# Two layers of a hybrid decoder on one core: the first stage of each layer with its ring of logits held in the banks

## The reference

```
h_n    = x * rsqrt(mean(x*x) + eps) * gain          # normalised rows
logits = einsum(q_idx, k_idx / 8)                   # 8 heads of 64, both rotated
score  = einsum(w * 8**-0.5, relu(logits))          # weighted sum over the 8 heads
idx    = top_k(where(causal, score, -inf), 128)
g      = -exp(a_log) * softplus(a + dt_bias);  gam = cumsum(g);  beta = sigmoid(b)
q,k,v  = silu(causal_conv(proj))                    # 4 taps
```

## Time and profile before

| | us |
|---|---|
| median of 3 runs (2298.42 to 2299.43) | 2298.96 |
| the profiled execution | 2299.94 |
| its span | 2298.2 |
| TensorE matmul busy | 2239.7 (97%) |
| VectorE busy | 1174.5 (51%) |
| ScalarE busy | 1000.6 (44%) |
| GpSimd busy | 1126.9 (49%) |

### The profile page before, as it was taken

One profiled execution on the slowest core, in us unless ns is written; L12 is line 12 of the kernel. 1 busy time (PEld: TensorE's weight loads), 2 busy tenths in 40 slices (PEclk: granted clock), 3 DMA queues, 4 the chain that ended last, 5 costly groups with the idle time before them and its releaser, 6 DMA issues.

```text
span 2298.2 us, 32941 instructions
## 1 busy us (share of the span) xinstructions
PE 2239.7 (97%) x12820; PEld 1834.3 (80%) x12820; DVE 1174.5 (51%) x2175; ACT 1000.6 (44%) x2237; POOL 1126.9 (49%) x824
## 2 busy tenths in 40 slices
PE   8999998999999999999999999999999999999998
PEld 6788887888788888888867888878887888888886
DVE  7778776544522344440186788754445324444302
ACT  5555655455522433332355455545544324333322
POOL 4366445333345555554445566443443555555542
PEclk9999999999999999999999999999999999999999
DMA  4211211222233333333322221112222333333332
GB/s 152 65 53 55 61 56 38 69 74 75 68 96 97 94 99 97 97 96 96 90 71 69 56 56 56 51 43 74 75 77 73 97 97 92 96 97 97 98 98 88
DMA packets 98939, 183.36 MB, mean 80 GB/s; under 512 B 11104, under 2 KB 11360, under 8 KB 98784
## 3 DMA queue, kind: packets, MB, share of 16 engines
q1 hardware_dynamic: 98784, 181.26, 27.3%
HBM read 179.12 MB, written 2.10 MB: 79 GB/s over the span
## 4 chain that ended last, share of the span: by engine, by line
PE 85%; DVE 10%; ACT 3%; issue 1%; POOL 1%; DMA 0%; DVEq 0%; SPq 0%; ACTq 0%; POOLq 0%
PE bank L1530 82%; PE bank L1597 2%; DVE conv_acc L1005 1%; DVE left L1005 1%; DVE normalised L1005 1%; PE bank L1875 1%; DVE bank L1002 1%; DVE ob_lo L1002 1%; ACT w_hi L596 1%; DVE left L1205 1%; POOL mt_even L535 0%; DVE iq L1002 0%; DVE inv L1002 0%; PE bank L1591 0%; ACT oa_hi L607 0%
## 5 line engine op out<-in xcount | busy, mean ns | idle before, releaser
L495 POOL TENSOR_TENSOR w_lo<-w_raw,w_hi 128x512 fp32r<-128x512 f32 x668 | 931.9, 1417 | 1071.9 <-ACT w_hi L596 1071.9
L1530 PE MATMUL bank<-xn_hi,w_lo 128*128 128x512 f32 x1840 | 747.5, 406 | 0.0
L1530 PE MATMUL bank<-xn_hi,w_hi 128*128 128x512 f32 x1840 | 739.1, 402 | 6.6 <-DVE conv_acc L1005 6.6
L1530 PE MATMUL bank<-xn_lo,w_hi 128*128 128x512 f32 x1840 | 731.0, 397 | 0.0
L596 ACT ACTIVATE w_hi<-w_raw 128x512 fp32r<-128x512 f32 x668 | 385.0, 624 | 653.6 <-PE bank L1530 648.9
L1530 PEld LDWEIGHTS bank<-xn_hi,w_hi 128*128 128x128 f32 x1840 | 348.0, 189 | 84.3 <-DVE conv_acc L1005 9.1
L1530 PEld LDWEIGHTS bank<-xn_hi,w_lo 128*128 128x128 f32 x1840 | 348.2, 189 | 72.5 <-issue 5.8
L1530 PEld LDWEIGHTS bank<-xn_lo,w_hi 128*128 128x128 f32 x1840 | 348.0, 189 | 68.5 <-issue 1.9
L1002 DVE TENSOR_TENSOR residual<-residual,bank 128x512 f32<-128x512 f32 x32 | 22.0, 686 | 252.8 <-PE bank L1530 252.4
L1530 PE MATMUL bank<-mid_hi,w_hi 128*128 128x512 f32 x352 | 136.9, 389 | 0.0
L1530 PE MATMUL bank<-mid_lo,w_hi 128*128 128x512 f32 x352 | 136.9, 389 | 0.0
(11 more groups left out here) (262 smaller groups left out, 3460.5 us busy)
## 6 DMA issues: line engine op xcount, KB each, us to landing
w_raw<-w_tiles SPq DMA_DIRECT2D x668, 256.0 KB, 2.6
residual<-x_t SPq DMA_DIRECT2D x4, 512.0 KB, 5.7
out_t<-normalised SPq DMA_DIRECT2D x8, 256.0 KB, 2.1
rope<-rope SPq DMA_DIRECT2D x2, 512.0 KB, 5.8
mats<-mats SPq DMA_DIRECT2D x1, 576.0 KB, 3.9
vecs_all<-vecs SPq DMA_DIRECT2D x1, 129.0 KB, 7.7
mats<-mats SPq DMA_DIRECT2D x1, 128.0 KB, 6.8
vecs_all<-vecs SPq DMA_DIRECT2D x1, 4.0 KB, 1.8
```

Source lines behind the costliest of these rows:

```text
L495: nc.gpsimd.tensor_tensor(w_lo[j][:], w_raw[j][:], w_hi[j][:].bitcast(F32), ALU.subtract).then_inc(s_lo, 1)
L1530: return nc.tensor.matmul(out, lhsT, rhs, start=start, stop=stop)
```

## The change

The buffers `irl` go. Relu now works in place in the bank, the adds read the bank, and TensorE waits for the add of the group before instead of its Relu. The keys of tile 0 go to bank 3 and the spread root to bank 0 (they change places). The normalised rows read the root from the bank instead of `row_r`; rows 0 and 2 are written to banks 4 and 5, and so the first logits wait for `lo2`. Front tile 0 (bank 0) waits for `y7`. Rows 6 and 7 and the adds of 512 columns in group 0 change places with other steps. The decays stand behind the adds of group 1 and convolution 1, Ln behind the tanh of convolution 1 and the tap of convolution 2, and TensorE issues 36 products instead of 6 before `cum`. Columns of the head and the masks follow convolution 3, the gate's row product follows convolution 5. Tile 0's products are issued half by half with all products of the high weight first (`low_last`), and at the start ScalarE makes the high copies 2 to 5 between the squares instead of ahead of them. Left out below are the lists of step names, which follow the new order, and lines in which only the bank's number changes.

```diff
 ab_col = sb("ab_col", [NC, 16], at=slot(42) + 512)
-irl = [sb(f"irl_{j}", [SEQ], at=slot(44 + j)) for j in range(HGROUP)]
...
+SPREAD, KEYS = 0, 3
...
+def scaled_in(k):
...
+    return bank[{0: 4, 2: 5}[k]][:] if k in (0, 2) else sq[:, k, :]
...
+def square_in(k):
...
+    return bank[SPREAD if k == KEYS else k][:]
...
     def square(k):
-        dst = squares[:, k, :] if k in (0, KD - 2) else bank[k][:]
+        dst = squares[:, k, :] if k in (0, KD - 2) else square_in(k)
...
             act.wait_ge(rms_v.sem, rms_v.after(turn, f"y{k}"))
-            copy(xn_hi[:, k, :], sq[:, k, :]).then_inc(rms_a.step(f"hi{k}"), 1)
+            copy(xn_hi[:, k, :], scaled_in(k)).then_inc(rms_a.step(f"hi{k}"), 1)
...
         def relus(g, t):
-            before = GROUPS.index((g, t)) - 1
             for i in heads_of(g):
-                j, n = i % HGROUP, (t + 1) * P
+                logit = bank[2 + i % HGROUP][:, :(t + 1) * P]
                 act.wait_ge(idx_p.sem, idx_p.after(l, f"lg{t}_{i}"))
-                if before >= 0:
-                    bg, bt = GROUPS[before]
-                    act.wait_ge(idx_v.sem, idx_v.after(l, f"acc{bt}_{bg * HGROUP + j}"))
-                nc.scalar.activation(irl[j][:, :n], bank[2 + j][:, :n], ACT.Relu).then_inc(idx_a.step(f"relu{t}_{i}"), 1)
+                nc.scalar.activation(logit, logit, ACT.Relu).then_inc(idx_a.step(f"relu{t}_{i}"), 1)
...
         w_hi_after(l, 4)
+        relus(0, 3)
         rms_hi(l, 6, 7)
-        relus(0, 3)
...
         relus(1, 1)
-        act.wait_ge(idx_v.sem, idx_v.after(l, "u"))
-        nc.scalar.activation(small[:, 7, :], small[:, 4, :], ACT.Ln).then_inc(idx_a.step("ln"), 1)
...
         relus(1, 3)
+        tile_done(l, T0_GDN + 2)
+        w_hi_after(l, T0_GDN + 2)
+        front_tanh(l, 0, 1)
+        front(l, 0, 2, False, split_next=False)
+        act.wait_ge(idx_v.sem, idx_v.after(l, "u"))
+        nc.scalar.activation(small[:, 7, :], small[:, 4, :], ACT.Ln).then_inc(idx_a.step("ln"), 1)
+        tile_done(l, T0_GDN + 3)
+        w_hi_after(l, T0_GDN + 3)
...
         nc.scalar.activation(col_total[:], small[:, 10, :].rearrange(by_head, c=NC), ACT.Exp).then_inc(idx_a.step("etot"), 1)
-        tile_done(l, T0_GDN + 2)
-        w_hi_after(l, T0_GDN + 2)
-        front_tanh(l, 0, 1)
-        front(l, 0, 2, False, split_next=False)
...
             w_hi_through(k // 3)
-    w_hi_through(3)
...
         square(k)
-        if k == 3:
-            w_hi_through(4)
+        if k % 2:
+            w_hi_through(2 + k // 2)
...
                 head_rest(l, 0)
-            tile_done(l, T0_GDN + m + 1)
-            w_hi_after(l, T0_GDN + m + 1)
+            if m > 2:
+                tile_done(l, T0_GDN + m + 1)
+                w_hi_after(l, T0_GDN + m + 1)
...
         into = KD - 2 if k == KD - 1 else 0
-        tt_(squares[:, into, :], squares[:, into, :], bank[k][:], ALU.add).then_inc(rms_v.step(f"sum{k}"), 1)
+        tt_(squares[:, into, :], squares[:, into, :], square_in(k), ALU.add).then_inc(rms_v.step(f"sum{k}"), 1)
...
         for k in which:
-            stt(sq[:, k, :], h[:, k, :], vec(l, V_MIX + k), row_r[:], ALU.mult, ALU.mult).then_inc(rms_v.step(f"y{k}"), 1)
+            stt(scaled_in(k), h[:, k, :], vec(l, V_MIX + k), bank[SPREAD][:], ALU.mult, ALU.mult).then_inc(rms_v.step(f"y{k}"), 1)
...
         dve.wait_ge(rms_a.sem, rms_a.after(l, f"hi{k}"))
-        tt_(xn_lo[:, k, :], sq[:, k, :], xn_hi[:, k, :].bitcast(F32), ALU.subtract).then_inc(rms_v.step(f"lo{k}"), 1)
+        tt_(xn_lo[:, k, :], scaled_in(k), xn_hi[:, k, :].bitcast(F32), ALU.subtract).then_inc(rms_v.step(f"lo{k}"), 1)
...
                 if i == 0:
-                    ins = V.tensor_scalar(left[t][:], irl[i % HGROUP][:, :n], w_col[:, t, 0:1], None, ALU.mult)
+                    ins = V.tensor_scalar(left[t][:], bank[2 + i % HGROUP][:, :n], w_col[:, t, 0:1], None, ALU.mult)
                 else:
-                    ins = stt(left[t][:], irl[i % HGROUP][:, :n], w_col[:, t, i:i + 1], left[t][:], ALU.mult, ALU.add)
+                    ins = stt(left[t][:], bank[2 + i % HGROUP][:, :n], w_col[:, t, i:i + 1], left[t][:], ALU.mult, ALU.add)
...
         turn_first("1", 7, iq[:, 2, :], tile(3))
+        scaled(l, 6, 7)
...
         accs(0, 2)
-        scaled(l, 6)
         turn_second("1", 7, 6, iq[:, 2, :], iq[:, 3, :], tile(4))
-        scaled(l, 7)
+        accs(0, 3)
         scaled_lo(l, 7)
-        accs(0, 3)
...
         tt_(sm(2), sm(0), sm(1), ALU.max).then_inc(idx_v.step("abs"), 1)
-        accs(1, 1)
+        for t in TOPK_TILES:
+            accs(1, t)
+        for what in ("t0_", "t1_", "t2_"):
+            front(l, 0, 1, what, False)
...
         V.reciprocal(sm(13), sm(12)).then_inc(idx_v.step("rden"), 1)
-        accs(1, 2)
...
         V.reciprocal(cols[:, :, 0, :], small[:, 8, :].rearrange("p (c h) -> p h c", c=NC)).then_inc(idx_v.step("beta"), 1)
-        accs(1, 3)
+        front(l, 0, 1, "silu", False)
         for what in ("t0_", "t1_", "t2_"):
-            front(l, 0, 1, what, False)
+            front(l, 0, 2, what, False)
...
         tt_(sm(11), sm(10), bank[7][:, :32], ALU.subtract).then_inc(idx_v.step("togo"), 1)
...
+    def index_masks(l):
...
             dve.wait_ge(idx_v.sem, idx_v.after(l, f"mask{t}"))
...
+    def gate_row(l):
...
         index(l)
-        front(l, 0, 1, "silu", False)
-        head_columns(l, 0)
-        for m in CV[1:-1]:
+        front(l, 0, 2, "silu", False)
+        for m in CV[2:-1]:
...
                 front(l, 0, m, what, False)
+            if m == CV[2]:
+                head_columns(l, 0)
+                index_masks(l)
+        gate_row(l)
...
-        def __init__(self, l, first, tiles, bank_free, x=None, x_ready=None, banks=dense):
+        def __init__(self, l, first, tiles, bank_free, x=None, x_ready=None, banks=dense, low_last=0):
...
             self.n = 0
+            self.low_last = low_last
...
                 m, k, p = n // (3 * KD), n // 3 % KD, n % 3
+                if m < self.low_last:
...
+                    at = n % (3 * HALF)
+                    k = n // (3 * HALF) % 2 * HALF + (at // 2 if at < 2 * HALF else at - 2 * HALF)
+                    p = 2 * (at % 2) if at < 2 * HALF else 1
+                    if k % HALF == 0:
+                        pe.wait_ge(*((s_lo, 2 * (self.l * TILES + self.first + m) + k // HALF + 1) if p == 1
+                                     else (s_hi, 2 * (self.l * TILES + self.first + m) + k // HALF + 1)))
...
                     self.bank_free(m)
-                if k % HALF == 0 and p == 0:
+                if k % HALF == 0 and p == 0 and m >= self.low_last:
...
                 ins = mm(self.banks[m % len(self.banks)][:], w[u % RING][:, k % HALF, :], (lo if p == 2 else hi)[:, k, :],
-                         start=(k == 0 and p == 0), stop=(k == KD - 1 and p == 2))
-                if k % HALF == HALF - 1 and p == 2:
+                         start=(k == 0 and p == 0), stop=n % (3 * KD) == 3 * KD - 1)
+                if n % (3 * HALF) == 3 * HALF - 1:
...
         def bank_free(m):
+            if m == 0 and l:
+                pe.wait_ge(dn_v.sem, dn_v.after(l - 1, f"h{KEYS}"))
...
-        e = Dense(l, 0, T_IDX, bank_free, lambda m: (un_hi, un_lo), x_ready, [bank[b] for b in (0, 6, 1, 7, 6)])
+        e = Dense(l, 0, T_IDX, bank_free, lambda m: (un_hi, un_lo), x_ready, [bank[b] for b in (KEYS, 6, 1, 7, 6)], low_last=1)
...
                         bg, bt = GROUPS[before]
-                        pe.wait_ge(idx_a.sem, idx_a.after(l, f"relu{bt}_{bg * HGROUP + i % HGROUP}"))
+                        pe.wait_ge(idx_v.sem, idx_v.after(l, f"acc{bt}_{bg * HGROUP + i % HGROUP}"))
...
         pe.wait_ge(idx_v.sem, idx_v.after(l, "rb0"))
-        pe.wait_ge(rms_a.sem, rms_a.after(l, "row"))
+        pe.wait_ge(idx_a.sem, idx_a.after(l, f"k1_{HGROUP - 1}"))
+        pe.wait_ge(rms_v.sem, rms_v.after(l, "lo2"))
...
         logits(1, 3)
-        d.issue(6)
+        d.issue(36)
...
             else:
-                pe.wait_ge(*((idx_v.sem, idx_v.after(l, "rb0")) if m else (idx_a.sem, idx_a.after(l, f"k1_{HGROUP - 1}"))))
+                pe.wait_ge(*((idx_v.sem, idx_v.after(l, "rb0")) if m else (rms_v.sem, rms_v.after(l, "y7"))))
...
             if i == 0:
-                pe.wait_ge(idx_a.sem, idx_a.after(l, of_group("relu", *GROUPS[-1])[-1]))
+                pe.wait_ge(idx_v.sem, idx_v.after(l, of_group("acc", *GROUPS[-1])[-1]))
...
                 down_products(m + lead, KF - 2)
-    pe.wait_ge(dn_v.sem, dn_v.after(DEPTH - 1, "h3"))
```

26 lines of the change are left out of this document (13 added, 13 removed).

## The result

| | before | after |
|---|---|---|
| median, us | 2298.69 (2297.47 to 2299.43, 4 runs) | 2286.22 (2285.93 to 2286.53, 4 runs) |
| ratio | | 0.9943, interval 0.9931 to 0.9955 |
| profiled execution / its span, us | 2299.94 / 2298.2 | 2286.3 / 2284.5 |
| VectorE busy, us | 1174.5 | 1151.4 |

The change is faster by 12.5 us. The forecast was 2285.5 in a range of 2280.0 to 2293.5.

The account below looks back on a forecast made before the run. TensorE was taken to bound the kernel, with a Relu stall that halves its clock; per layer 13.1 us removed less 5.6 added, minus 1.15 for first logits, plus 1.5 once at the start, gave 14.2 off 2299.94: forecast 2285.5, range 2280.0 to 2293.5.

Parts of the forecast that it names:

- The stall and its clock: TensorE's 3.3 us wait for a Relu plus slow products at half clock behind it: 7.8 us a layer removed.
- Banks for the adds: VectorE's ring adds reading a bank would take 0.5, 0.64 and 0.76 us for 256, 384 and 512 columns.
- Logits, group 0: TensorE's first logits group: no wait at 384 columns, 0.4 us lost at 512 because the adds of 384 end late.
- The wait for the decays: TensorE idles before its running sums, since the decays now stand behind convolution 1: 2.2 us a layer added.
- The convolution waits: TensorE's remaining waits at tiles 3 to 6 and the next pair's tile 0: 2.5 us a layer.
- The wait for `lo2`: First logits wait for the second subtraction because normalised rows 0 and 2 lie in banks: 1.15 us a layer.
- The start: Layer 0 only: low weights last and earlier sums of squares end the token sums 1.5 us earlier.
- The signs: Expected in the profile: no Relu wait, start below 7 us, given logits and add durations, no half clock past the start.
- Rival A: The idle wait for the decays drops TensorE's clock: about 4 us a layer, 2293.5 with both layers, 2289.5 with one; chance 0.22.
- Rival B: The stall only moves: 512-column adds of group 0 stay late, TensorE idles over 3 us, 2301, no change; chance 0.05.
- Rival C: Slower: adds from a bank cost what disturbed ones did, 15.5 us a layer in the single-buffered ring, 2316.7; chance 0.04.
- D: At the start, low weights last save nothing as tile 0 waits for its low inputs: costs 1.5, 2287; with forecast 0.69.

Follow-up runs that it names:

- SBUF run: The changed kernel with the Relu result written to an SBUF buffer and the adds reading there, bank still held until the add: 2291.82 us, ratio 0.9965.
- the decays in front: The changed kernel with the decays, Ln and exponentials back ahead of convolution 1 and 6 products before `cum`: 2281.29 us, ratio 0.9921.
- twelve more products: The changed kernel with 48 ring products instead of 36 issued ahead of the cumulative decays on TensorE: 2289.43 us, ratio 0.9956.
- old-order version: The changed kernel with normalised rows 6 and 7 and their high copies back in the old order around the 512-column logits of group 0: 2289.25 us, ratio 0.9956.

## Why the prediction was right, point by point

- **The stall and its clock, 7.8 a layer:** gone in both layers, as said. But the sum credited them as if anything that removes them gained 7.8. Filled with idle work, the old kernel gave 0.7 a layer. The step holds only together with VectorE's relief, which the prediction priced apart. The Relu wait came back too, with 2.1 us, when the old ring stood in the new order.
- **Banks for the adds:** taken at 0.5, 0.64 and 0.76; measured 0.51, 0.64 (1.93 for three at 43.86) and 0.77. The SBUF run shows its worth where the bank is held until the add, 5.6 us in all by the medians and 7.2 by the ruler; against the whole old ring in the new order it is 2.0 a layer where the clock stayed and 5.0 where it fell. The prediction put the slow normalised rows down to their place as well, but in the kernel before the row at 51.63 us took 0.75 from SBUF, while GpSimd was idle.
- **Logits, group 0:** 384 without a wait (1.57, right); 512 were to lose 0.4 and lost 0.8 (2.82 against 2.00). **Group 1:** 384 were to lose 0.5 and lost nothing (1.67); 512 lost 0.2 (2.22). In sum 1.0 against 0.9.
- **The wait for the decays:** 2.2 forecast, 1.9 measured.
- **The convolution waits:** 2.5 forecast, 2.4 measured (0.32, 0.92 and 1.20; the 0.3 for tile 4 didn't come).
- **Refilling the array:** a term left out. The sum removed 0.15 for each of four old breaks and charged nothing for the four new ones, the waits at 70.23, 75.13, 85.15 and 104.77 us. In the rows such a break costs 0.16 on top of the wait shown, while the last product runs out (0.39 against 0.23 to the next start), and 0.11 behind it, more than the 0.15, but it cancels between old and new. At the sum's own price the new ones make 0.6. With that, 13.1 - (1.0 + 1.9 + 2.4 + 0.6) is 7.2, and from the first logits to the next pair's first tile the trace has 7.17 in layer 0 and 7.15 in layer 1, against 7.5.
- **The wait for `lo2`:** 1.15 forecast; 1.04 measured in the wait, 1.10 and 1.11 in the two layers' timelines. Right in size, but the run with the rows in SBUF shows that it wasn't a loss: most of it comes back at the next two banks.
- **The start, 1.5:** wrong, 0.43 in this execution and 0.3 in the mean. The failed step is "the sum of squares is the next thing late". VectorE's last sum ended at 19.49, not 18.5, and TensorE had begun the token sums at 18.91, straight behind its product at 18.68, without waiting for it; with the decays in front the last square ended at 17.83, as forecast, and the token sums started at 19.63.

  What held TensorE up were its own first products and the third weight remainder. The first products lie 0.43 us apart in both kernels, up to 13.4 us here and 14.3 before, at a granted clock that reads 1.00; why isn't shown. From there on they follow every 0.23 us, and 0.9 of the 1.5 us is left. The wait for the third remainder at 16.06 takes some 0.45 more. This remainder, forecast to begin at 13.6, began at 14.7, since its high copy stands behind two squares and those behind copies that waited for loads (0.58 and 0.61 us). In the run with the low weights not last it ended at 16.00 too, and tile 1 started at 16.06 in both, which is why the token sums agree to the hundredth. GpSimd, TensorE and VectorE of the change:

```profile
14.72 1.29 POOL L504 TENSOR_TENSOR w_lo<-w_raw,w_hi 128x512 fp32r<-128x512 f32 x1 [3.53 <-ACT w_hi L605]
...
16.06 0.50 PE L1544 MATMUL bank<-un_hi,w_hi 128*128 128x512 f32 x1 [0.17 <-POOL w_lo L504]
...
18.68 0.39 PE L1544 MATMUL bank<-un_lo,w_hi 128*128 128x512 f32 x1
...
18.80 0.69 DVE L1008 TENSOR_TENSOR squares<-squares,bank 128x512 f32<-128x512 f32 x1 [0.58 <-ACT bank L620]
```

- **What wasn't foreseen:** 0.6 us more a layer inside the DeltaNet of pair 0 (6.50 us ahead at the next pair's first tile, 7.07 at the transposes of `tt_both`). The products on `q_f` are 6.48 ahead and the transposes 7.07, so it arises between them, where VectorE's `a_t` had waited 3.74 us for GpSimd's `decay` and now waits 3.21 for TensorE. No run isolates it.
- **The sum:** 14.2 forecast, 13.7 measured. The two misses, 1.1 at the start and 1.2 in the refills of two layers, were nearly made up by the DeltaNet's extra, 1.2, and by waits that came out 0.3 a layer shorter than forecast. That the total fits to 0.5 is in part luck.
- **The signs:** those of the ring came, the start below 7 us (6.66) and adds of 512 columns at 0.77 among them, but for the logits of 512 columns (2.82 and 2.22 against 2.0). "No slice at clock 0.50 past the start" did not: the clock fell in front of both attentions, as it had in the kernel before.
- **Rival A,** 0.22, did not come in the changed kernel's rings but in four of its neighbours (rows in the old place, low weights not last, rows in SBUF, twelve more products), behind the same wait or the one that takes its place. So its chance was not too high, but its price was: 4 us a layer forecast, about 1.6 measured (88.79 against 90.35 us with the low weights not last, where only layer 1 lost the clock). The low clock lasted 3.4 us there (1203.7 to 1207.1), not the 8 that the prediction had charged.
- **Rival B** came true of the old kernel with its Relus moved, not of the change. **Rival C** did not come: adds of 256 columns took 0.51 from a bank beside a busy GpSimd, not the disturbed 1.12. **D** was right in its number, as the low weights last save next to nothing, but hardly in its reason: tile 0 waited only 0.30 us for its low inputs.
- **The rule on PSUM operands.** The first operation of a group took 0.75 us for 512 columns from a bank and 0.48 from SBUF, 0.61 and 0.41 for 384. The Trainium skill (VectorE: DVE Perf Modes, "Why PSUM operands drop a tier") says that an fp32 operand in PSUM can't have the doubled rate; the traces agree. It costs 0.27 us an instruction at 512 columns, against 0.6 that each disturbed SBUF add of 256 columns lost.

## What to carry to other kernels

A stall on the busiest engine has the length that the profile shows, but its worth is what is left when the next engine in the ring is late too; fill it with idle work once, and the difference (here 4.5 us expected and 0.7 got) tells whose pace it is. Where two engines meet at SBUF, look at an operation's duration beside the other engine before counting instructions: moving one operand into a bank halved the adds that ran beside GpSimd. Test the order and the place apart: here the new order alone brought 4.1 of the 6 us where the clock stayed, and 1.0 where it fell. And when two versions differ by a gap in TensorE of about 2 us, compare them by a stretch of the timeline, since the clock falls behind such a gap in some executions and not in others and moves a median by several us.

## What the runs showed of the hardware that was not expected

- The granted clock behind a gap of about 2 us is not settled by the gap: 1.89 us kept it in the change and lost it in the old-order version; 2.10 kept it in layer 0 and 2.09 lost it in layer 1 of the same execution; 1.09 and 1.52 us, close together, kept it in one execution and lost it in another of the same kernel. The shortest gap with a fall behind it was 0.94 us, in front of the token sums of the old kernel with its Relus first (0.50 from 21.3 to 24.7 us). What decides was not found. The Trainium skill (TensorE: Matmul & The Clock Gate, "What's actually happening") says that the gate's window runs freely and isn't aligned to the kernel; that would make the same gap fall differently from execution to execution, and no run here can show it. A fall behind the wait for the decays cost about 1.6 us; one in front of the attention 1.4 us where it lasted 3.4 us and 2.35 where it lasted 6.8; one behind a Relu wait 3.1 us (93.73 against 90.68).
- VectorE's three adds of 256 columns took 1.52 us with one operand in a bank and 3.32 to 3.35 with both in SBUF. The stretches of the SBUF version and of the change beside them; POOL is the fifth engine:

```profile
38.40:41.80 3.40, 2.90 (x13) 1.56 (x11) 3.26 (x4) 0.80 (x2) 2.55 (x2) 1.00 0.18 58
```

```profile
38.50:40.10 1.60, 1.60 (x9) 1.29 (x8) 1.46 (x5) 1.37 (x4) 1.60 (x2) 1.00 0.00 0
```

GpSimd is busy in both, and only the SBUF adds suffer. Where it was idle (49.7 to 51.6 us in the kernel before), three SBUF adds of 384 columns took 1.93 us, as from the banks. No run took GpSimd's work away, so that it is the disturber is argued from these stretches. The Trainium skill (SBUF — State Buffer, "Who interferes with whom") says that a VectorE operation with two SBUF inputs contends with a GpSimd operation that reads SBUF, over a pair of ports that the two share, and that one with at most one SBUF input does not. The rows agree.
